# Cross attention's scores as three products of rounded high and low parts, the parts made by ScalarE and VectorE

## The reference, cut to what matters

```
q = (h @ wq).reshape(B, T, X_HEADS, X_HEAD_DIM)      # 512 tokens, 4 heads of 256
k = (m @ wk).reshape(B, M, X_HEADS, X_HEAD_DIM)      # 256 memory positions
s = jnp.einsum('bthd,bmhd->bhtm', q, k) * (X_HEAD_DIM ** -0.5)
p = jax.nn.softmax(s, axis=-1)
```

## Time and profile before

| | us |
|---|---|
| median of 3 runs | 1740.92 (1740.75 to 1741.7) |
| the profiled execution | 1740.76 |
| its span, first to last instruction | 1738.9 |
| TensorE busy | 1701.5 (98% of the span) |
| VectorE, ScalarE, GpSimd busy | 681.1, 589.5, 710.9 |
| granted TensorE clock, mean | 0.996 of full |

### The profile page before, as it was taken

One profiled execution on the slowest core, in us unless ns is written; L12 is line 12 of the kernel. 1 busy time (PEld: TensorE's weight loads), 2 busy tenths in 40 slices (PEclk: granted clock), 3 DMA queues, 4 the chain that ended last, 5 costly groups with the idle time before them and its releaser, 6 DMA issues.

```text
span 1738.9 us, 21093 instructions
## 1 busy us (share of the span) xinstructions
PE 1701.5 (98%) x8525; PEld 1417.6 (82%) x8525; DVE 681.1 (39%) x1122; ACT 589.5 (34%) x890; POOL 710.9 (41%) x386
## 2 busy tenths in 40 slices
PE   7999999998999999999999999999899999999998
PEld 6888888897888789879888888898657988888886
DVE  3111211268776776356211121266884522112122
ACT  4222222256444554236222222246453422222210
POOL 3443444445554343114453444433331454444442
PEclk9999999999999999999999999999999999999999
DMA  6333243333222345212433233342111333323322
GB/s 189 97 97 97 79 116 97 97 110 85 61 61 61 97 125 142 73 49 71 112 97 97 82 112 97 86 128 61 37 37 49 85 98 97 97 82 112 97 85 73
DMA packets 302826, 157.66 MB, mean 91 GB/s; under 512 B 5145, under 2 KB 301194, under 8 KB 302730
## 3 DMA queue, kind: packets, MB, share of 16 engines
q1 hardware_dynamic: 302730, 156.32, 31.6%
HBM read 154.20 MB, written 2.10 MB: 90 GB/s over the span
## 4 chain that ended last, share of the span: by engine, by line
PE 66%; DVE 4%; ACT 3%; issue 2%; POOL 0%; DVEq 0%; ACTq 0%; POOLq 0%
PE bank L434 16%; PE bank L435 16%; PE bank L438 15%; PE bank L2430 1%; PE bank L2054 1%; PE bank L2051 1%; PE bank L2050 1%; PE bank L481 1%; PE bank L482 1%; PE bank L486 1%; PE bank L2206 1%; PE bank L467 1%; PE bank L461 1%; PE bank L462 1%; PE bank L2311 1%
## 5 line engine op out<-in xcount | busy, mean ns | idle before, releaser
L399 POOL TENSOR_TENSOR wlo<-wraw,whi 128x1024 fp32r<-128x1024 f32 (+1 forms) x256 | 608.6, 2390 | 909.9 <-ACT whi L394 909.9
L434 PE MATMUL bank<-ahi,whi 128*128 128x512 f32 x1312 | 516.0, 393 | 0.0
L435 PE MATMUL bank<-alo,whi 128*128 128x512 f32 x1312 | 511.7, 390 | 0.0
L394 ACT CAST whi<-wraw 128x1024 fp32r<-128x1024 f32 (+1 forms) x286 | 285.9, 1025 | 255.4 <-PE bank L438 169.4
L438 PE MATMUL bank<-ahi,wlo 128*128 128x512 f32 x1312 | 324.0, 389 | 0.0
L434 PEld LDWEIGHTS bank<-ahi,whi 128*128 128x128 f32 x1312 | 247.2, 188 | 52.1 <-issue 1.2
L435 PEld LDWEIGHTS bank<-alo,whi 128*128 128x128 f32 x1312 | 247.0, 188 | 52.0 <-issue 1.2
L438 PEld LDWEIGHTS bank<-ahi,wlo 128*128 128x128 f32 x1312 | 246.3, 188 | 51.1
L1377 DVE SCALAR_TENSOR_TENSOR hval<-gate,bank 128x512 f32<-128x512 f32 x66 | 45.4, 688 | 557.2 <-PE bank L438 543.2
L859 ACT ACTIVATE gate<-bank 128x512 f32<-128x512 f32 x66 | 39.6, 600 | 514.9 <-PE bank L438 506.1
L1386 DVE SCALAR_TENSOR_TENSOR res<-res,bank 128x512 f32<-128x512 f32 x80 | 54.1, 686 | 261.7 <-PE bank L438 181.7
(11 more groups left out here) (304 smaller groups left out, 2241.7 us busy)
## 6 DMA issues: line engine op xcount, KB each, us to landing
wraw<-in_ffn_w_gate SPq DMA_DIRECT2D x44, 512.0 KB, 3.8
wraw<-in_ffn_w_up SPq DMA_DIRECT2D x44, 512.0 KB, 3.8
wraw<-in_w_in SPq DMA_DIRECT2D x34, 512.0 KB, 3.9
wraw<-in_ffn_w_down SPq DMA_DIRECT2D x32, 512.0 KB, 4.0
wraw<-in_w_gate SPq DMA_DIRECT2D x22, 512.0 KB, 3.8
wraw<-in_w_up SPq DMA_DIRECT2D x22, 512.0 KB, 3.8
wraw<-in_w_out SPq DMA_DIRECT2D x16, 512.0 KB, 4.4
wraw<-in_w_down SPq DMA_DIRECT2D x16, 512.0 KB, 4.0
```

The lines of the kernel that those rows point to most:

```text
L394: eng.copy(whi[:, b % 4, 0:n], wraw[:, b % RAW, 0:n]).then_inc(hi_ready, 1)
L399: eng.tensor_tensor(wlo[:, b % RAW, 0:n], wraw[:, b % RAW, 0:n], whi[:, b % 4, 0:n], ALU.subtract).then_inc(LO[b][0], 1)
L434: eng.matmul(o, w, xhi[:, k, :], start=(k == 0), stop=False)
L435: eng.matmul(o, w, xlo[:, k, :], start=False, stop=False)
```

## The change

- `qx` and `kx` give way to `qxhi`, `qxlo`, `kxhi`, `kxlo` in fp32r. The factor 1/16 moves from the queries to the keys. The buffers lie elsewhere in the working area.
- ScalarE makes the high parts from the banks: `key_hi(m - 1)` at the head of step m of its `mk`/`mv` loop, ahead of the cast of the step's weight block and of `second_norm`; `query_hi(j - 1)` in step j of `xq`, and the last one behind the loop.
- VectorE makes the low parts in the places of its two copies. They now wait for ScalarE's high part (two new semaphores) in place of the finished block, and it is they that free the bank.
- In ScalarE's share of the norm, the wait for the variance with the logarithm and exponential moves from m == 2 to m == 3.
- `cross_scores` issues 24 products of 256 columns a head, three for each of the 8 before.

```diff
@@
+        kxhi = take("kxhi", [P, KD, MEM], F32R)
+        qxhi = take("qxhi", [P, KD, T], F32R)
+        qxlo = take("qxlo", [P, KD, T], F32R)
+        kxlo = take("kxlo", [P, KD, MEM], F32R)
@@ ScalarE, second_norm
                 if m == 2:
                     act.wait_ge(stat_mean, 1)
                     act.activation(var[:, 0, :], mean_of("ln2"), ACT.Square).then_inc(mean_sq, 1)
+                if m == 3:
                     act.wait_ge(var_ready, 1)
@@ ScalarE
+            def key_hi(j):
+                wait_block(act, phases["mk"], j)
+                act.activation(kxhi[:, j, :], bank_of(phases["mk"], j)[:, 0:MEM], ACT.Identity, scale=(D // XH) ** -0.5).then_inc(s_kxh, 1)
+
+            def query_hi(j):
+                wait_block(act, phases["xq"], j)
+                act.copy(qxhi[:, j, :], bank_of(phases["xq"], j)[:, :]).then_inc(s_qxh, 1)
+
             for m in range(2 * KD):
+                if 1 <= m <= KD:
+                    key_hi(m - 1)
                 hi_stream(phases["mk"], m)
                 second_norm(m)
@@
             for j in range(KD):
                 hi_stream(phases["xq"], j)
                 second_norm(2 * KD + j)
+                if j:
+                    query_hi(j - 1)
                 if j == 5:
                     cross_exp(0)
+            query_hi(KD - 1)
@@ VectorE
             for j in range(KD):
-                wait_block(dve, phases["mk"], j)
-                dve.tensor_copy(kx[:, j, :], bank_of(phases["mk"], j)[:, 0:MEM]).then_inc(bank_free, 1)
+                dve.wait_ge(s_kxh, j + 1)
+                dve.scalar_tensor_tensor(out=kxlo[:, j, :], in0=bank_of(phases["mk"], j)[:, 0:MEM], scalar=(D // XH) ** -0.5,
+                                         in1=kxhi[:, j, :], op0=ALU.mult, op1=ALU.subtract).then_inc(bank_free, 1)
@@
-                wait_block(dve, phases["xq"], j)
-
-                dve.tensor_scalar(qx[:, j, :], bank_of(phases["xq"], j)[:, :], (D // XH) ** -0.5, None, ALU.mult).then_inc(bank_free, 1)
+                dve.wait_ge(s_qxh, j + 1)
+                dve.tensor_tensor(qxlo[:, j, :], bank_of(phases["xq"], j)[:, :], qxhi[:, j, :], ALU.subtract).then_inc(bank_free, 1)
@@ TensorE, cross_scores
-                    for k in range(2):
-                        i = pe.matmul(bank[SCORE_BANK[h] + t // 2][:, (t % 2) * MEM:(t % 2 + 1) * MEM],
-                                      qx[:, 2 * h + k, t * P:(t + 1) * P], kx[:, 2 * h + k, :], start=(k == 0), stop=(k == 1))
+                    for k in range(2 * h, 2 * h + 2):
+                        pe.matmul(o, qxhi[:, k, at], kxhi[:, k, :], start=(k == 2 * h), stop=False)
+                        pe.matmul(o, qxhi[:, k, at], kxlo[:, k, :], start=False, stop=False)
+                        i = pe.matmul(o, qxlo[:, k, at], kxhi[:, k, :], start=False, stop=(k == 2 * h + 1))
```

More of the change, by code:

```diff
@@ L196, in build @@
         mval = take("mval", [P, MVAL, MEM])
-        kx = take("kx", [P, KD, MEM])
+        vxt = take("vxt", [P, 2, MEM])
+        kxhi = take("kxhi", [P, KD, MEM], F32R)
         vx = take("vx", [P, MT, D])
-        vxt = take("vxt", [P, 2, MEM])
-        take = region(WORK + 48 * KB)
-        qx = take("qx", [P, KD, T])
+        qxhi = take("qxhi", [P, KD, T], F32R)
+        qxlo = take("qxlo", [P, KD, T], F32R)
+        kxlo = take("kxlo", [P, KD, MEM], F32R)
         take = region(WORK)
@@ L628, in build @@
         s_ah = sem("attended_hi")
+        s_kxh = sem("memory_keys_hi")
+        s_qxh = sem("memory_queries_hi")
         s_rope = sem("rope_loaded")
@@ L2309, in cross_scores @@
                 for t in range(TT):
-                    for k in range(2):
-                        i = pe.matmul(bank[SCORE_BANK[h] + t // 2][:, (t % 2) * MEM:(t % 2 + 1) * MEM],
-                                      qx[:, 2 * h + k, t * P:(t + 1) * P], kx[:, 2 * h + k, :], start=(k == 0), stop=(k == 1))
+                    o, at = bank[SCORE_BANK[h] + t // 2][:, (t % 2) * MEM:(t % 2 + 1) * MEM], slice(t * P, (t + 1) * P)
+                    for k in range(2 * h, 2 * h + 2):
+                        pe.matmul(o, qxhi[:, k, at], kxhi[:, k, :], start=(k == 2 * h), stop=False)
+                        pe.matmul(o, qxhi[:, k, at], kxlo[:, k, :], start=False, stop=False)
+                        i = pe.matmul(o, qxlo[:, k, at], kxhi[:, k, :], start=False, stop=(k == 2 * h + 1))
                 i.then_inc(s_sc, 1)
```

## The result

The changed kernel takes 1743.85 us, the median of 22 runs (1740.99 to 1744.65); the kernel before, run beside it, 1740.88 us (22 runs, 1740.16 to 1742.3). The ratio is 1.0014, with a 95% interval of 1.0009 to 1.002: 2.4 us slower, 1.6 to 3.5. (The medians alone differ by 2.97 us; the ratios of this document are not quotients of two medians.) That is real and still inside what the prediction called no change. The forecast was 1742.3 us. The range held, but the time lies above the forecast's own bracket (1741.2 to 1743.4), so one term is missing from its sum.

The account below looks back on a forecast made before the run. TensorE, busy 98% of the span, was taken as the bound. Savings of 1.4 us and a stall of 2.8 gave +1.4 on 1738.9, so 1740.3; with 1.9 around it 1742.2, forecast as 1742.3 us, range 1739.1 to 1744.6.

Parts of the forecast that it names:

- the forecast's own bracket: Whole kernel: a stall of 2 to 3.6 us and a saving of 1.0 to 1.8, 1741.2 to 1743.4 us; chance 0.58.
- The products: Scores: 24 rounded products at 0.119 us, 2.85 us a head instead of 3.45; head 0's 0.6 us gained whole.
- The 0.05 us taken off for the change of format: Attention: 0.05 us deducted from the gain for the format change behind the float32 transposes.
- The attention: From turn 0 to turn 3: shorter scores start the VectorE/ScalarE chain earlier, gaining 0.8 us.
- and turn 3 with them: Attention: head 3's maxima come 0.6 + 0.23 = 0.83 us earlier, and turn 3 by as much.
- the predicted waits: Attention: TensorE would wait about 0.4 us in front of attend 1 and 1.1 in front of turn 3.
- The collision: Key phase: GpSimd's low part holds the shared port lock, so VectorE's clamp ends at 643.4 instead of 641.45.
- the stall: Start of mv: TensorE idle 2.8 us (bounds 0 to 3.6), waiting for VectorE's low part queued behind kxlo.
- the third rival: Behind the idle time at mv: the clock falls to half, costing 1.7 to 3.4 us more, 1744.0 to 1745.7; chance 0.12.
- a sign of being wrong: Key phase: a clock of 0.50 behind the idle time at mv's start would count against the forecast.
- the choice between two rows: Clock: 0.50 after 4.12 us idle, 1.00 after 3.42, so a fall was expected from about 4 us on.
- Within 0.2%: Whole kernel: a time from 1737.4 to 1744.4 us, within 3.5 us, counts as the same; chance 0.85.

Follow-up runs that it names:

- psum_var: Changed kernel with the variance difference left in its PSUM bank, so VectorE's clamp reads PSUM instead of SBUF; ratio 0.9996 to the kernel before.
- lo_first: Changed kernel with VectorE's low part of the weights put ahead of its wait for ScalarE's high part of the keys in mk; ratio 0.9994 to the kernel before.
- both: Changed kernel with the clamp reading PSUM and VectorE's low part of the weights ahead of the wait in mk; ratio 0.999 to the kernel before.
- h_only: Changed kernel with its handoffs kept but the scores multiplied as full float32, eight instructions a head; ratio 1.0024 to the kernel before.
- late_two_23: Changed kernel with keys split at the start of xq, and the low query x high key product left out for heads 2 and 3; ratio 0.9997.
- late_reorder: Changed kernel with keys split at the start of xq, and head 0's attended low part moved behind head 3's maxima and turn 2's copy; 1737.74 us.
- var_delay: Changed kernel with the clamp reading PSUM, plus two useless VectorE operations ahead of kxlo 6; ratio 1.0028 to the kernel before.

## Why the prediction was right, and where not

- **The products.** 0.119 us apiece was taken over from the trace and 0.120 found; head 0 gained 0.59 for 0.6. Right. The 0.05 us taken off for the change of format had no row behind it; the traces show 0.08 at such a place (the first rounded product behind turn 1 starts at 738.83, the next at 739.03, 0.20 later in place of 0.12).
- **The attention.** -0.8 was forecast and -0.57 measured. Head 3's maxima did come earlier as worked out: they start 15.59 us behind turn 0 before (741.23 - 725.64) and 14.70 after (742.83 - 728.13), 0.89 gained. The step that failed is "and turn 3 with them". Head 3's exponentials are queued on ScalarE behind its copy of turn 2, and turn 2 waits for VectorE's copy of turn 1. Before the change TensorE's scores 3 hid that wait: the copy of turn 1 ended at 741.00, scores 3 at 741.19. Of the predicted waits, 0.4 us in front of attend 1 and 1.1 in front of turn 3, neither came where it was put: there are 1.08 us in front of turn 2 and 0.46 in front of turn 3, the latter no different from before. Reordering VectorE removed the first one, and 1.2 us with it.
- **The collision and the stall.** The clamp was forecast at 1.9 us and took 1.91; the idle time in front of `mv` at 2.8, and the stall is 2.79. psum_var and lo_first take away one of the two named causes each, both takes away the two. Right, with its mechanism.
- **The clock.** This is the term that was missing: +1.50 us, nearly the whole difference between the forecast (1742.3) and the median (1743.85). It was the third rival, with a chance of 0.12, and the prediction had named a clock of 0.50 behind the stall as a sign of being wrong. The step that failed is the choice between two rows: 0.50 after 4.12 us of idle time, 1.00 after 3.42; hence "from a stall of about 4 us on". One held clock at 3.42 is no bound, and the trace of before contradicted it 9 us earlier, at a place that the prediction doesn't weigh. TensorE's records there, and two windows:

```profile
1252.87 1.77 PE L2418 MATMUL bank<-mats,ps 128*128 128x128 f32 x8 [1.09 <-DVE ps L1912]
```
```profile
1252.00:1254.00 2.00, 1.13 (x6) 1.13 (x7) 2.00 (x4) 0.55 (x1) 1.92 (x3) 0.78 0.00 0
1254.00:1256.00 2.00, 2.00 (x7) 1.65 (x7) 1.08 (x3) 1.37 (x5) 1.92 (x2) 0.50 0.00 0
```

  Two waits of 0.88 and 1.09 us, 2.2 us apart, had been enough there. The same trace has another such place: ahead of 489.29 and 491.62 TensorE waited for 1.01 and 0.33 us, and from 492 to 494 the clock was 0.50. So the trace of before already spoke for a higher chance of this rival. The size of the rival was roughly right where it was bracketed from below: 1.7 us for 3.4 us at half clock; 1.50 came.
- **The chances.** "Within 0.2%" had 0.85, and +2.4 us (at most +3.5) is within. But the likeliest single number was 1.5 us low, and a rival at 0.12 was what happened. That the range held owes something to luck: it was meant to leave out most of the clock's cases, put at 1744.0 to 1745.7. The clock's case came, and cheaper (1.5 us) than its bracket of 1.7 to 3.4.

## What to carry to other kernels

When work is split so that a second engine waits for a first, look at what stands in the second one's queue behind that wait: here it was the operand that the bound engine needs next, and putting it ahead of the wait, with a source in PSUM for one small operation, gave back all 4.3 us. Time taken from the bound engine is only gained up to the next link in somebody else's queue, and what is saved beyond it piles up as idle time that can cost clock as well. Price a new idle time of TensorE with the half clock that may follow it, some 1.5 us here, and give it a real chance: in the two stretches changed here it came after each of the four idle times of 2.6 us or more. That is no rule, for near 1260 us it also stayed away after 3.4 to 3.6 us.

## What the runs showed of the hardware

- TensorE's granted clock and the idle time before it don't go together by length alone. Behind 1.43 us in front of `mv` it stayed 1.00; behind 2.63, 2.62, 4.27 (in front of `mv`) and 2.99 (turn 2 without two heads' products) it was 0.50. But the same pair of places near 1250 and 1260 us of every kernel gave three outcomes. In the kernel before it fell behind the wait of 1.09 and held behind the one of 3.42; in psum_var it held at the first and fell at the second; in h_only (1.06 and 3.56 us) it held at both. Over all 13 kernels there is an order in it: in the four where it fell at the first place (before, changed, lo_first, late_two_23) it held at the second, behind 3.41 to 3.44 us, and in eight of the nine where it held at the first it fell at the second, in seven of them during the wait of 3.56 to 3.58 us or within half a microsecond behind it, and in late_reorder 1.4 us behind it. So the held clock on which the prediction leaned followed a fall 9 us before it. psum_var's records, and a window at the second:

```profile
1253.60 1.09 PE L2437 MATMUL bank<-mats,ps 128*128 128x128 f32 x8 [1.07 <-DVE ps L1929]
1261.30 1.97 PE L2437 MATMUL bank<-mats,ps 128*128 128x128 f32 x8 [3.57 <-DVE ps L1929]
```
```profile
1260.00:1262.00 2.00, 0.70 (x4) 0.70 (x4) 1.97 (x4) 0.92 (x3) 1.86 (x2) 0.50 0.00 0
```

  What decides at the first place stays open; it was not tried.
- Executions of one kernel differ by more than the steps studied here. The executions of psum_var lie from 1738.3 to 1739.0 us (five, mean granted clock 0.996) and from 1741.1 to 1742.9 (six, 0.993 to 0.996), though the one profiled, of 1742.9, kept its clock in front of `mv` and lost it near 1260 us; whether that makes the two groups wasn't measured. That the clock falls behind the changed kernel's stall was seen in its one profile and in that of h_only. In how many of its executions it falls wasn't measured; the medians' 2.97 us against the trace's 3.13 suggest most of them.
- After the fall the clock stayed low for about 3.4 us in the changed kernel and for more than 6 in var_delay (from 653.7 to about 660), where TensorE had stood idle for longer at the low level.
- Of VectorE and GpSimd, whoever started first made the other one wait, where both worked from SBUF. In var_delay a lead of 0.02 us was enough for GpSimd: VectorE's 1.22 us became 3.40. Where VectorE was first by more than half a microsecond, its own length was unchanged and GpSimd's 2.41 became 2.84. An operation of VectorE that reads a bank (0.69 us) ran unhindered under GpSimd's, although alone it is the slower form (0.43 from SBUF).
